# High and low parts of an activation tile side by side, read as four streams in turns, with the meta norm moved

## The reference

```
h    = rmsnorm(x, pre_mix_g)
proj = h @ w_in                              # q, k, v of three attentions, and three gates
ga, gb, gc = sigmoid(g + b_gate)             # 3 x 2048 columns
mix  = ga*(ya @ w_oa) + gb*(yb @ w_ob) + gc*(yc @ w_oc)
x    = x + rmsnorm(mix @ w_out, post_mix_g)
h    = rmsnorm(x, pre_ffn_g)
u    = h @ w_up                              # 2048 -> 2 x 5632, then a causal conv of width 3
x    = x + rmsnorm((gelu(gate) * val) @ w_down, post_ffn_g)
```

## Time and profile before

| | us |
|---|---|
| median of 3 runs | 2176.36 (2176.31 to 2176.39) |
| span of the profiled execution | 2174.5 |
| TensorE busy in it | 2146.3 (99%) |
| VectorE busy | 1515.7 (70%) |
| ScalarE busy | 1192.1 (55%) |
| GpSimd busy | 220.4 (10%) |

### The profile page before, as it was taken

One profiled execution on the slowest core, in us unless ns is written; L12 is line 12 of the kernel. 1 busy time (PEld: TensorE's weight loads), 2 busy tenths in 40 slices (PEclk: granted clock), 3 DMA queues, 4 the chain that ended last, 5 costly groups with the idle time before them and its releaser, 6 DMA issues.

```text
span 2174.5 us, 38978 instructions
## 1 busy us (share of the span) xinstructions
PE 2146.3 (99%) x14559; PEld 1988.1 (91%) x14559; DVE 1515.7 (70%) x2075; ACT 1192.1 (55%) x1788; POOL 220.4 (10%) x146
## 2 busy tenths in 40 slices
PE   9999999999999999999999999999999999999998
PEld 8888899999889999999988889999889999999987
DVE  6676765668578888888855556999666565567755
ACT  5455654545455545555544446555666565676553
POOL 0000000000003223232300000221000000012110
PEclk9999999999999999999999999999999999999999
DMA  8655566657656576666666665665345647555454
GB/s 292 198 156 162 160 202 209 198 171 238 213 157 205 182 220 187 210 198 188 217 200 204 203 202 171 195 191 189 118 118 179 183 142 235 171 160 146 136 203 156
DMA packets 259011, 405.59 MB, mean 187 GB/s; under 512 B 16671, under 2 KB 115868, under 8 KB 257852
## 3 DMA queue, kind: packets, MB, share of 16 engines
q1 hardware_dynamic: 257204, 396.87, 58.8%
q10 hardware_dynamic: 1688, 7.07, 0.9%
HBM read 396.32 MB, written 4.22 MB: 184 GB/s over the span
## 4 chain that ended last, share of the span: by engine, by line
PE 90%; DVE 5%; ACT 3%; issue 1%; DMA 0%; DVEq 0%; ACTq 0%; SPq 0%
PE bank L2304 29%; PE bank L2300 23%; PE bank L2413 14%; PE bank L2297 12%; PE bank L2896 3%; PE bank L2319 2%; DVE wboth L1388 1%; ACT wboth L706 1%; PE bank L2643 1%; PE bank L2865 1%; PE bank L2821 1%; PE bank L2615 1%; DVE xtok L1542 0%; PE bank L2681 0%; PE bank L2348 0%
## 5 line engine op out<-in xcount | busy, mean ns | idle before, releaser
L1388 DVE TENSOR_TENSOR wboth<-raw,wboth 128x1024 fp32r<-128x1024 f32 (+1 forms) x748 | 909.2, 1228 | 516.5 <-ACT wboth L706 513.5
L706 ACT ACTIVATE wboth<-raw 128x1024 fp32r<-128x1024 f32 (+1 forms) x748 | 770.8, 1039 | 609.9 <-PE bank L2300 263.5
L2300 PE MATMUL bank<-aboth,wboth 128*128 128x512 f32 x2496 | 812.8, 382 | 2.3 <-DVE aboth L1607 1.1
L2297 PE MATMUL bank<-aboth,wboth 128*128 128x256 f32 x2496 | 659.2, 274 | 1.0 <-DVE wboth L1388 1.0
L2304 PE MATMUL bank<-aboth,wboth 128*128 128x272 f32 (+1 forms) x5184 | 624.0, 280 | 4.6 <-DVE aboth L1607 3.1
L2304 PEld LDWEIGHTS bank<-aboth,wboth 128*128 128x128 f32 x5184 | 606.1, 190 | 8.4 <-issue 3.9
L2300 PEld LDWEIGHTS bank<-aboth,wboth 128*128 128x128 f32 x2496 | 462.4, 190 | 59.9 <-issue 1.6
L2297 PEld LDWEIGHTS bank<-aboth,wboth 128*128 128x128 f32 x2496 | 478.4, 192 | 12.6 <-issue 2.7
L2413 PE MATMUL bank<-wboth,ghi 128*128 128x512 f32 x704 | 210.0, 380 | 0.9 <-DVE wboth L1388 0.9
L2924 POOL CAST ghi<-pr 128x256 f32 x44 | 84.3, 1917 | 691.2 <-DVE pr L1876 691.2
L2413 PEld LDWEIGHTS bank<-wboth,ghi 128*128 128x128 f32 x704 | 133.3, 189 | 19.9 <-DVE wboth L1388 1.3
(11 more groups left out here) (373 smaller groups left out, 1874.3 us busy)
## 6 DMA issues: line engine op xcount, KB each, us to landing
raw<-in_w_up SPq DMA_DIRECT2D x176, 512.0 KB, 4.6
raw<-in_w_in SPq DMA_DIRECT2D x156, 512.0 KB, 4.5
raw<-in_attn_w_in SPq DMA_DIRECT2D x96, 512.0 KB, 4.1
raw<-in_gla_w_in SPq DMA_DIRECT2D x96, 512.0 KB, 3.9
raw<-in_w_down SPq DMA_DIRECT2D x80, 512.0 KB, 4.6
raw<-in_w_out SPq DMA_DIRECT2D x32, 512.0 KB, 4.3
raw<-in_attn_w_out SPq DMA_DIRECT2D x32, 512.0 KB, 3.9
raw<-in_gla_w_out SPq DMA_DIRECT2D x32, 512.0 KB, 4.1
```

The source lines that it names most:

```text
L706: act.activation(whi[:, u % RING, 0:c], raw[:, u % RAW, 0:c], ACT.Copy).then_inc(whi_ready, 1)
L1388: dve.tensor_tensor(wlo[:, u % RING, 0:c], raw[:, u % RAW, 0:c], whi[:, u % RING, 0:c].bitcast(F32), ALU.subtract).then_inc(wlo_ready, 1)
L2297: mm = pe.matmul(bank[:, base + t, 0:T], w[1][:, k, col:col + P], in_turns(rhs(0, k0 + k)), start=False, stop=False)
L2300: mm = pe.matmul(bank[:, base + t, 0:2 * T], w[0][:, k, col:col + P], parts_in_turns(both(k0 + k)), start=first, stop=last)
```

## The change

`aboth` becomes [16 tiles][640 columns]. For the second block nothing changes but the step: a tile's high part has columns 0 to 319, its low part 320 to 639. The first block puts the low part right behind the 256 high columns, in 256 to 511 (`alo_beside`). A tile's four streams (high 0 to 127, high 128 to 255, low, low) are then 128 columns apart each, and the 512-column product reads all four in turns. The order of the 512 columns in the bank changes with it: a token's high and low sums lie two columns apart. So the 256-column product writes pairs of columns, four apart (`first_of_parts`), and `parts_together` joins by the new order.

Since `alo_beside` covers the columns 256 to 271 of the high part, the meta norm can't be written during `wout`. It moves to `down`'s first pass, units 9 to 13, with a wait of ScalarE for `up`'s last products (its scratch is `cv`'s space) and one of TensorE for `up`'s last bank. `yn2` and `gain2` now share each tile's 640 columns.

```diff
-        aboth = sb("aboth", [P, 2, KD * AS], F32R)
-        ahi, alo = aboth[:, 0, :], aboth[:, 1, :]
+        aboth = sb("aboth", [P, KD, 2 * AS], F32R)
+        ahi, alo, alo_beside = aboth[:, :, 0:AS], aboth[:, :, AS:2 * AS], aboth[:, :, TB:2 * TB]
...
         def parts_in_turns(ap):
-            return ap.rearrange("p s (h c) -> p s c h", h=2)
+            return ap.rearrange("p (q c) -> p c q", q=4)
 
         def parts_together(ap):
-            return ap.rearrange("p (s c h) -> p h c s", s=2, h=2)
+            return ap.rearrange("p (c s h) -> p h c s", s=2, h=2)
+
+        def first_of_parts(ap):
+            return ap.rearrange("p (c s h) -> p s c h", s=2, h=2)[:, 0, :, :]
 
         def ha(t, k, c0, n):
-            return t[:, k * AS + c0:k * AS + c0 + n]
+            return t[:, k, c0:c0 + n]
...
-        yn2 = sb("yn2", [P, KD, AS], at_=YN_AT[2])
-        gain2 = sb("gain2", [P, KD, AS], at_=GAIN_AT[2])
+        yngain2 = sb("yn2", [P, KD, 2 * AS], at_=act_at)
+        yn2, gain2 = yngain2[:, :, 0:AS], yngain2[:, :, AS:2 * AS]
...
             def model_parts(k):
-                return aboth[:, :, k * AS:k * AS + TB]
+                return aboth[:, k, 0:2 * TB]
...
                                 if of_weight:
-                                    mm = pe.matmul(bank[:, base + t, 0:T], w[1][:, k, col:col + P], in_turns(rhs(0, k0 + k)),
+                                    mm = pe.matmul(first_of_parts(bank[:, base + t, :]), w[1][:, k, col:col + P], in_turns(rhs(0, k0 + k)),
                                                    start=False, stop=False)
...
             for i in range(TRIPS["down"]):
                 for j in range(UNITS["down"]):
                     rows_of_unit("down", 2, i, j)
+                    if (i, j) == (0, 10):
+                        pe.wait_ge(acc_free, 4 * C0["down"])
+                        meta_mean(0)
...
+            def beside_first_down(i, j):
+                if j == 9:
+                    act.wait_ge(ff_prod, FT)
+                    meta_square(0, xm[:, :, :])
+                if j == 11:
+                    meta_root(0)
+                if j == 13:
+                    meta_hi(0)
+                if j == 28:
+                    rows_moments(2, 0)
```

More of the change, by code:

```diff
@@ L247, in two_blocks_kernel @@
         mixtmp = sb("mixtmp", [P, 2, 4, TB], F32, at_=bias_at + N_HEADS * TB * 4 + 24 * TB * 4)
-        YN_AT = [None, R2, act_at, R2 + 4 * KD * T2]
-        GAIN_AT = [None, R2 + 4 * 2 * D, act_at + 4 * KD * AS, R2 + 4 * (KD * T2 + 2 * D)]
+        YN_AT = [None, R2, None, R2 + 4 * KD * T2]
+        GAIN_AT = [None, R2 + 4 * 2 * D, None, R2 + 4 * (KD * T2 + 2 * D)]
         XN_AT = [R2, R2 + 4 * 3 * D, R2 + 4 * (24 * T2 + 3 * 1024), R2 + 4 * (16 * T2 + 3 * D)]
@@ L494, in meta_columns @@
         def meta_columns(t):
-            return t[:, :].rearrange("p (k t) -> p k t", t=AS)[:, :, TB:T2]
+            return t[:, :, TB:T2]
         def over_meta(ap):
@@ L586, in four_tiles @@
         def four_tiles(t, group):
-            return t[:, :].rearrange("p (k t) -> p k t", t=AS)[:, 4 * group:4 * group + 4, 0:TB]
+            return t[:, 4 * group:4 * group + 4, 0:TB]
         def ring_waits(eng, ph, i, u, n, landed):
@@ L1050, in beside_wout @@
                     mix_high(KD // 4 - 1)
[L1051 to L1056, removed]
             for i in range(TRIPS["wout"]):
@@ L1082, in _ @@
             down_rows = rows_out_of(2)
-            trip("down", 0, down_rows, after=lambda i, j: rows_moments(2, 0) if j == 28 else None)
+            def beside_first_down(i, j):
[8 more added lines that the diff above has]
+                    rows_moments(2, 0)
+            trip("down", 0, down_rows, after=beside_first_down)
             trip("down", 1, down_rows, after=lambda i, j: rows_moments(2, j // 24 + 1) if j in (4, 28) else None, held=1)
@@ L1354, in _ @@
                 act.wait_ge(z3_ready, h + 1)
-                zhi = ahi[:, :].rearrange("p (k t) -> p k t", t=AS)[:, 4 * h:4 * h + 4, 0:TB]
+                zhi = four_tiles(ahi, h)
                 act.activation(zhi, gg[:, 4 * h:4 * h + 4, :], ACT.Copy).then_inc(z3hi, 1)
@@ L1431, in first_lo @@
                 for k in (2 * g, 2 * g + 1):
-                    dve.scalar_tensor_tensor(ha(alo, k, 0, TB), turned(k), column("pre_mix_g", k), ha(ahi, k, 0, TB).bitcast(F32),
+                    dve.scalar_tensor_tensor(ha(alo_beside, k, 0, TB), turned(k), column("pre_mix_g", k), ha(ahi, k, 0, TB).bitcast(F32),
                                              ALU.mult, ALU.subtract).then_inc(act_ready, 1)
@@ L1606, in norm_lo @@
                 for k in (2 * g, 2 * g + 1):
-                    dve.scalar_tensor_tensor(ha(alo, k, 0, TB), turned(k), par[:, G_PRE[b] + k:G_PRE[b] + k + 1],
+                    dve.scalar_tensor_tensor(ha(alo_beside if b == 1 else alo, k, 0, TB), turned(k), par[:, G_PRE[b] + k:G_PRE[b] + k + 1],
                                              ha(ahi, k, 0, TB).bitcast(F32), ALU.mult, ALU.subtract).then_inc(act_ready, 1)
@@ L1813, in mix_low @@
                 dve.wait_ge(mix_hi, group + 1)
-                dve.tensor_tensor(four_tiles(alo, group), mixtmp[:, 0, :, :], four_tiles(ahi, group).bitcast(F32), ALU.subtract)\
+                dve.tensor_tensor(four_tiles(alo_beside, group), mixtmp[:, 0, :, :], four_tiles(ahi, group).bitcast(F32), ALU.subtract)\
                    .then_inc(act_ready, 4)
@@ L1826, in beside_wout @@
                     mix_low(KD // 4 - 1)
[L1827 to L1832, removed]
             for i in range(TRIPS["wout"]):
@@ L1887, in beside_down @@
                     rows_crossed(2, c)
+                if (i, j) == (0, 9):
+                    meta_sum(0)
+                if (i, j) == (0, 12):
+                    meta_norm(0, 2)
+                if (i, j) == (0, 13):
+                    meta_lo(1)
                 if (i, j) == (1, 36):
@@ L2318, in tokens @@
                         for wp, ap in PASSES:
-                            mm = pe.matmul(bank[:, first_bank + tt, 0:cols[1] - cols[0]], ha((ahi, alo)[ap], k0 + k, tt * P, P),
+                            mm = pe.matmul(bank[:, first_bank + tt, 0:cols[1] - cols[0]], ha((ahi, alo_beside)[ap], k0 + k, tt * P, P),
                                            in_turns(w[wp][:, k, cols[0]:cols[1]]),
@@ L2401, in rows_of_unit @@
                 w = [t[:, u % RING, :].rearrange("p (k n) -> p k n", k=2 if nk == 1 else nk) for t in (whi, wlo)]
-                src = (ahi, alo) if b == 1 else (ghi, glo)
+                src = (ahi, alo_beside) if b == 1 else (ghi, glo)
                 for tt in range(2):
@@ L2535, in _ @@
                         if of_weight:
-                            mm = pe.matmul(bank[:, 0, 0:TB], w[1][:, k, 0:P], in_turns(ha(ahi, k0 + k, 0, TB)), start=False, stop=False)
+                            mm = pe.matmul(first_of_parts(bank[:, 0, :]), w[1][:, k, 0:P], in_turns(ha(ahi, k0 + k, 0, TB)), start=False, stop=False)
                         else:
@@ L2547, in _ @@
                             if of_low:
-                                mm = pe.matmul(bank[:, 1 + tt, 0:P], ha(alo, k0 + k, tt * P, P), whi[:, u % RING, c0:c0 + P],
+                                mm = pe.matmul(bank[:, 1 + tt, 0:P], ha(alo_beside, k0 + k, tt * P, P), whi[:, u % RING, c0:c0 + P],
                                                start=False, stop=False)
@@ L2572, in _ @@
                     rows_of_unit("wout", 1, i, j)
-                    if (i, j) == (0, 10):
-                        meta_mean(0)
             keep_busy(1, 12)
@@ L2955, in _ @@
                 pool.wait_ge(z3hi, h + 1)
-                tiles = [t[:, :].rearrange("p (k t) -> p k t", t=AS)[:, 4 * h:4 * h + 4, 0:TB] for t in (alo, ahi)]
+                tiles = [four_tiles(t, h) for t in (alo, ahi)]
                 if h == 1:
```

## The result

The changed kernel takes 2318.11 us (median of 4 runs, 2317.79 to 2318.22) against 2176.38 us before (4 runs), a ratio of 1.065 with a 95% interval of 1.0637 to 1.0662. The forecast was 2176.4 us with a range to 2191.

The account below looks back on a forecast made before the run. TensorE, never idle in the gates and up projection, was taken to bound the kernel through the spacing of its products. The terms summed to 0 - 0.22 + 0.22 = 0, giving 2176.4 us, with a range from 2174 to 2191 us.

Parts of the forecast that it names:

- The read of the 512-column product: Line 2300, 2512 products: four streams in turns instead of two, taken as 0 between -6.3 and +536 us.
- Rival 2: Line 2300: four streams are read too slowly, from +6.3 us (one more start) to +536 us; chance 0.14.
- twice the only fixed part the rows show: Basis of the range's upper end: losses of up to 6 ns a product, 15 us above 2176.4 us.
- The write term: 256-column product, line 2297: writing 128 pairs 16 bytes apart costs 0, at most 262 us at half rate.
- The reading of before: Gates before the change: a pair takes 215.8 + 111.7 = 327.5 ns; the layout costs nothing, except perhaps 2.5 ns.
- My last sign: Gates and up projection: a unit distance away from 2.62 us would prove the reading of today's unit times wrong.
- the reading of rows 4 to 7: From unit times in gates, down projection, branch outputs and second block: the layout has no cost now and gets none.
- Rival 1: 512-column product: four streams return the 2.5 ns above its column time, -6.3 us to 2170.1 us; chance 0.24.
- a 256-column product's slot is its weight load: TensorE: the next product's weight load starts with this 256-column product, which is as short; the next starts 0.11 us later.
- The joins: VectorE, line 1843, gates and projections: adding elements 8 bytes apart instead of 1024 costs 0, staying at 683 ns.
- the meta norm: Its small TensorE product leaves the output projection (-0.22 us) and returns in the down projection's first pass (+0.22): 0.
- added wait: ScalarE's and TensorE's new waits for the up projection's last work cost nothing; ScalarE's has 17 us of slack.

Follow-up runs that it names:

- e2_read_or_write: Changed kernel, gates read two streams but write stepped pairs, up projection reads four but the bank holds the old order: 2275.97 us; gates 2.62, up 3.10 us a unit.
- e1_order_back: Changed kernel with only the order of columns put back, layout and moved norm kept: 2176.45 us against 2176.62 us before the change, ratio 1.000.

## Why the prediction was wrong

**The step that failed** is "*The read of the 512-column product*", where I took 0 between -6.3 and +536 us. It is the term that was mis-sized: 59.6 ns for each of 1104 products and 59.0 for each of the 1408 in the up projection make 149 us. The whole is 142 us, or 56.5 ns a product. When the n-th product of one trace is set beside the n-th of the other, the missing 7 us fall at 100 to 133 us and 200 to 270 us of the kernel before (2.4 and 2.3 us), in the first pass of the up projection (about 1.7) and at the step into the down projection (0.7). TensorE had idle time around three of these before (2.3, 2.1 and 2.7 us in the windows 40 to 130, 200 to 300 and 600 to 660 us); that the longer products cover part of such waits fits this and was not tested. What misled me was "the row nearest to it is the two-stream read": two streams at two distances say that these distances are harmless to two streams, and I took them to say that the number is. Of one, two, four and eight streams only two ran at 2.62 us a unit. Rival 2 was the right mechanism in the right place ("nothing covers it"), with a chance of 0.14 placed near its small end of +6 us, and the range was cut at 6 ns a product on the strength of "twice the only fixed part the rows show", a figure from products of two streams that says nothing of four. With ends as far apart as 0 and 536 us and no row with four streams, the range was too narrow.

**What counts in the read** is the order and the places, by the runs. Moving the low part by 16 bytes leaves a unit at 3.04 us, and moving it by 8 brings it to 2.72. Reading neighbouring columns one after the other is not what helps: one stream, which does so throughout, is slower (2.83 us a unit) than two in turns (2.62), and four in turns range from 2.70 to 3.12 over the same columns.

**The write term, 0, held.** `e2_read_or_write` has it by itself: 2.62 us a unit with both products stepped. The rows that I gave for it were weak, since rows 10 compare two different operations of VectorE reading PSUM, and none of TensorE writing it. A step that breaks the pairs was not run.

**The reading of before held**: a pair is 215.8 + 111.7 ns, and no order that was tried returned any of it. Its 2.4 GHz is not in the clock row, which gives tenths of full speed; it follows from rows 5 and 7, where 240 more columns (512 for 272) take 100.0 ns more, 0.417 ns each. My last sign was too wide: a unit away from 2.62 us disproves "gets none", the cost of the new order, and leaves the reading of rows 4 to 7 standing. Rival 1 (four streams return the 2.5 ns) is dead; the best four-stream setting (2.70 us a unit) is 10 ns slower. That a 256-column product's slot is its weight load stays an inference.

**The joins, 0, held** (682 ns for 683), **the meta norm, -0.22 + 0.22, held** (2.81 us gone from the output projection, 2.82 in the down projection), and neither added wait shows. `e1_order_back` holds all three and the new tile step in one figure: ratio 1.000.

## What to carry to other kernels

When TensorE is never idle, price an operand's access pattern by a row that has the same pattern; where no row has it, one run with the pattern in a single phase is worth more than any nearest row, because the cost multiplies with every product (59 ns became 142 us here). Put two patterns into two phases of one kernel and read the distance between conversions: that gave two measurements a run here. Of the reads run here on fp32r operands at a granted clock of 0.998 or 0.999, two streams in turns were the fastest: 2.62 us a unit, against 2.83 with one stream, 2.70 to 3.12 with four over both parts and 5.41 with eight.

## What the runs showed of the hardware that was not expected

- One stream read straight through costs 353 ns a pair (2.83 us a unit), two in turns 327.5 (2.62): the obvious pattern is 8% slower than the twisted one.
- Two streams in turns take 2.62 us a unit both at 512 bytes apart, where they enter new pieces in neighbouring columns, and at 520, where they don't.
- Eight streams in turns, four for the 256-column product: 5.41 us a unit, more than twice the 2.62 of two streams.
- Which of equal settings is 3.04, 3.10 or 3.12 us depends on the distances too (1040 and 1056 bytes: 3.04; 1024 and 1280: 3.10). This stays open.
